# First attention of a two-block kernel: stacked head pairs and score products on 64 rows each

## The reference, cut to what matters

```
qa = partial_rope(rms_norm(q_a.reshape(B, S, 8, 64), moba_q_norm[l]), positions)
ka = partial_rope(rms_norm(k_a.reshape(B, S, 8, 64), moba_k_norm[l]), positions)
s_own = jnp.einsum('bhqd,bhld->bhql', qi, k_own) * 64 ** -0.5
s_own = jnp.where(kpos[None, :] <= qpos[:, None], s_own, -jnp.inf)
p = jax.nn.softmax(s_own, axis=-1)
o_a = jnp.einsum('bhql,bhld->bhqd', p, v)
```

## Time and profile before

| | |
|---|---|
| median of 3 runs | 1429.86 us (1429.76 to 1430.22) |
| span of the profiled execution | 1426.4 us |
| PE busy | 1393.7 us, 98% |
| DVE busy | 990.3 us, 69% |
| ACT busy | 753.3 us, 53% |
| chain that ended last | PE 86%, DVE 7%, ACT 4% |
| mean granted TensorE clock | 0.998 |

### The profile page before, as it was taken

How to read it: one execution, slowest core, us unless ns; L and a number is a source line. 1 busy time by engine, 2 the same in 40 slices (tenths; PEclk the granted TensorE clock), 3 DMA queues, 4 the chain that set the end, 5 groups by cost and what they waited for, 6 DMA issues and landing times.

```text
span 1426.4 us, 18882 instructions
## 1 busy us (share of the span) xinstructions
PE 1393.7 (98%) x7575; PEld 1194.3 (84%) x7575; DVE 990.3 (69%) x1201; ACT 753.3 (53%) x1061; POOL 60.0 (4%) x46
## 2 busy tenths in 40 slices
PE   7999999999999999999999999999999999999998
PEld 6988888988887988898877888879788987788886
DVE  6689777698766679647776565457795568665553
ACT  6764766764764575434454443356743445444432
POOL 2002000002000000000000000000100000000000
PEclk9999999999999999999999999999999999999999
DMA  8544345544333654324445555454533334375553
GB/s 302 189 147 148 96 136 181 175 140 143 108 119 125 236 193 147 119 100 151 143 153 177 178 185 179 154 211 157 199 119 119 108 134 157 118 227 186 177 178 117
DMA packets 139125, 225.72 MB, mean 158 GB/s; under 512 B 8032, under 2 KB 54432, under 8 KB 138912
## 3 DMA queue, kind: packets, MB, share of 16 engines
q1 hardware_dynamic: 137376, 221.90, 46.3%
q10 hardware_dynamic: 1664, 2.63, 0.5%
HBM read 223.46 MB, written 1.05 MB: 157 GB/s over the span
## 4 chain that ended last, share of the span: by engine, by line
PE 86%; DVE 7%; ACT 4%; issue 1%; DMA 1%; POOL 1%; SPq 0%; ACTq 0%; DVEq 0%
PE gp L577 63%; PE gp L566 7%; PE mp L847 5%; PE mp L549 4%; DVE wt_rest L1423 2%; PE mp L684 2%; DVE arena L1417 1%; PE mp L738 1%; DVE arena L1885 1%; POOL rs_out L2130 1%; PE mp L840 1%; PE mp L712 1%; PE mp L698 0%; ACT first_hi L1035 0%; ACT arena L1272 0%
## 5 line engine op out<-in xcount | busy, mean ns | idle before, releaser
L1423 DVE TENSOR_TENSOR wt_rest<-wt,wt_hi 128x1024 fp32r<-128x1024 f32 x156 | 184.0, 1221 | 75.1 <-ACT wt_hi L1035 74.3
L1035 ACT ACTIVATE wt_hi<-wt 128x1024 fp32r<-128x1024 f32 x156 | 156.7, 1054 | 101.0 <-DMA wt<-in_ffn_up 49.7
L1423 DVE TENSOR_TENSOR wt_rest<-wt,mix_hi 128x1024 fp32r<-128x1024 f32 x136 | 160.6, 1221 | 57.9 <-ACT mix_hi L1035 56.9
L1035 ACT ACTIVATE mix_hi<-wt 128x1024 fp32r<-128x1024 f32 x136 | 139.6, 1061 | 101.3 <-PE gp L577 57.0
L577 PE MATMUL gp<-wt_rest,mix_hT_hi 128*128 128x512 f32 x384 | 149.6, 390 | 0.0
L577 PE MATMUL gp<-wt_hi,hT_hi 128*128 128x512 f32 x352 | 140.3, 398 | 4.8 <-DVE wt_rest L1423 4.0
L577 PE MATMUL gp<-mix_hi,mix_hT_hi 128*128 128x512 f32 x352 | 140.6, 399 | 4.1 <-DVE wt_rest L1423 3.0
L577 PE MATMUL gp<-wt_hi,hT_rest 128*128 128x512 f32 x352 | 137.4, 390 | 0.0
L577 PE MATMUL gp<-mix_hi,mix_hT_rest 128*128 128x512 f32 x352 | 137.2, 390 | 0.0
L577 PE MATMUL gp<-wt_rest,hT_hi 128*128 128x512 f32 x352 | 137.1, 390 | 0.0
L1035 ACT ACTIVATE first_hi<-wt 128x1024 fp32r<-128x1024 f32 x104 | 106.4, 1061 | 47.8 <-PE gp L577 36.4
(11 more groups left out here) (320 smaller groups left out, 3028.4 us busy)
## 6 DMA issues: line engine op xcount, KB each, us to landing
wt<-in_w_in SPq DMA_DIRECT2D x100, 1024.0 KB, 4.9
wt<-in_ffn_gate SPq DMA_DIRECT2D x44, 512.0 KB, 3.7
wt<-in_ffn_up SPq DMA_DIRECT2D x44, 512.0 KB, 4.8
wt<-in_w_out SPq DMA_DIRECT2D x20, 1024.0 KB, 4.9
wt<-in_ffn_down SPq DMA_DIRECT2D x20, 1024.0 KB, 4.9
wt<-in_w_mem_kv SPq DMA_DIRECT2D x8, 1024.0 KB, 6.0
wt<-in_w_branch_pool SPq DMA_DIRECT2D x4, 1024.0 KB, 5.0
wt<-in_w_branch_ret SPq DMA_DIRECT2D x4, 1024.0 KB, 5.0
```

Source lines behind the costliest of these rows:

```text
L1035: nc.scalar.activation(rounded_part(u)[:, k:k + nk, :], wt[:, u % SLOTS, k:k + nk, :], ACT.Copy)\
L1423: return nc.vector.tensor_tensor(o, i0, i1, ALU.subtract)
```

## The change

QT gets the layout of KT: 4 pairs, even head in partitions 0 to 63, odd head in 64 to 127, no zeros. ACT copies it in two instructions of 128 partitions in place of four of 64. POOL's zero fill of QT is gone. A score product takes the 64 partitions of its own head, queries and keys. `scores` works on a pair: it begins both heads' steps (the waits of both stand ahead of the first product), then does t = 0 of the even head, t = 0 of the odd head, t = 1 of the even head, t = 1 of the odd head. The order of the steps and of everything else is as before.

```diff
-        QT, KT = region(a_QT, NH_A, S), region(a_KT, 4, S)
+        QT, KT = region(a_QT, 4, S), region(a_KT, 4, S)
...
-                def scores(h):
-                    begin(s(f"sc{h}"), read_out(s("kaT0")), read_out(s("kaT1")), read_out(s("qaT0")), read_out(s("qaT1")))
-                    b = bank(s(f"sc{h}"))
-                    nc.tensor.matmul(b[:, 0:P], QT[:, h, 0:P], KT[:, h // 2, 0:P], start=True, stop=True)
-                    end(nc.tensor.matmul(b[:, P:3 * P], QT[:, h, P:S], KT[:, h // 2, :], start=True, stop=True))
+                def scores(pair):
+                    for h in (2 * pair, 2 * pair + 1):
+                        begin(s(f"sc{h}"), read_out(s("kaT0")), read_out(s("kaT1")), read_out(s("qaT0")), read_out(s("qaT1")))
+                    for t in range(TT):
+                        for h in (2 * pair, 2 * pair + 1):
+                            rows = slice(DH_A * (h % 2), DH_A * (h % 2) + DH_A)
+                            o = bank(s(f"sc{h}"))[:, P * t:P * t + P * (t + 1)]
+                            ins = nc.tensor.matmul(o, QT[rows, pair, P * t:P * t + P], KT[rows, pair, 0:P * (t + 1)], start=True, stop=True)
+                            if t == TT - 1:
+                                end(ins)
...
-                for h in range(4):
-                    scores(h)
+                for pair in range(2):
+                    scores(pair)
                 y_transposes(2)
                 split_units(s("Z0"), 1)
-                for h in range(4, 8):
-                    scores(h)
+                for pair in range(2, 4):
+                    scores(pair)
                 split_units(s("Z0"), 1)
...
-                for t in range(TT):
-                    st = s(f"qaT{t}")
-                    act.wait_ge(*computed(st))
-                    nc.scalar.activation(QT[0:64, 0:8:2, t * P:t * P + P], bank(st, 4, P)[0:64], ACT.Copy)
-                    nc.scalar.activation(QT[64:128, 1:8:2, t * P:t * P + P], bank(st, 4, P)[64:128], ACT.Copy).then_inc(step_read[STEP_NO[st] % 4], 1)
-                for t in range(TT):
-                    evacuate(f"kaT{t}", KT[:, :, t * P:t * P + P], bank(s(f"kaT{t}"), 4, P))
+                for n, dst in (("qaT", QT), ("kaT", KT)):
+                    for t in range(TT):
+                        evacuate(f"{n}{t}", dst[:, :, t * P:t * P + P], bank(s(f"{n}{t}"), 4, P))
...
-            nc.gpsimd.memset(QT, 0.0)
```

## The result

| | before | changed |
|---|---|---|
| median, first comparison | 1429.81 us (4 runs) | 1435.04 us (4 runs, 1434.78 to 1435.70) |
| ratio | | 1.0039, 95% interval 1.0024 to 1.0053 |
| span of the profiled execution | 1426.4 us | 1432.8 us |
| PE, DVE, ACT, POOL busy | 1393.7, 990.3, 753.3, 60.0 | 1394.5, 990.3, 750.4, 59.1 |

The account below looks back on a forecast made before the run. PE was taken as the bound (busy 98%, 86% of the chain). After the last bank's release, 0.11 + 0.88 + 0.10 = 1.09 us against 0.76, +0.33 a layer, +0.7 in two: 1429.86 to 1430.5 us; range 1429.0 to 1432.3.

Parts of the forecast that it names:

- Where the products stand: Scores of heads 0 to 5 lie beside ACT's work; PE's 1.40 us a layer saved there becomes wait.
- ACT's copies and POOL's fill at nothing: ACT's 1.37 us a layer ends in its waits for PE; POOL's 1.80 us at the start is off the path: 0.
- The pair: Two heads' score products on separate halves, partly overlapping, rows starting in order: 0.88 us on PE.
- The middle of my bounds: Pair time of 0.88 us, between 0.66 with perfect overlap and 1.31 with none.
- The change of form: Tile form back from 64 to 128 rows behind heads 6 and 7: 0.10 us a layer, ends 0 and 0.31.
- The order of the waits: Heads 6 and 7 start only when both banks are free, at 178.40 as before; 1.09 us after release, before 0.76.
- The high end of my range: After the release, no overlap and large change of form: 0.11 + 1.31 + 0.31 = 1.73 us, +0.97 a layer.
- The clock: Granted clock behind PE's wait before heads 6 and 7: the sum kept it at 1.00, adding nothing.
- the rival: Longer wait halves the clock behind heads 6 and 7: 1.45 us a layer, 1433.4; chance 0.07 both layers, 0.03 one.

Follow-up runs that it names:

- e11: The changed kernel with POOL's zero fill of the query region put back at the start; 1434.90 us, ratio 1.0034 to before.
- e10: The changed kernel with scores head after head again, each head with its own waits and its own 64 rows; 1432.71 us, ratio 1.0021 to before.
- e2: The changed kernel with six extra full products, results unused, between heads 5 and 6; 1430.87 us, ratio 1.0010 to before.
- e9: The changed kernel with query and key waits only at head 0 and six unused full products between heads 5 and 6; 1429.56 us, ratio 1.0000 to before.
- e3: The changed kernel with the query and key waits only at head 0, not at all eight heads; 1432.28 us, ratio 1.0019 to before.
- e14: As e9, but two full filler products before heads 6 and 7 instead of six; 1431.95 us, ratio 1.0015 to before.
- e5: The kernel before, its 128-row products in the change's order of waits and products, executed once more for a trace; 1434.66 us (1 run).
- e12: As e9, but the six filler products use only the lower 64 rows; 1430.05 us, ratio 1.0003 to before.

## Why the prediction was wrong

**Where the products stand.** Right. The first five or six heads lie beside ACT's work, and all that PE saved there became wait: 5.0 us in two layers.

**ACT's copies and POOL's fill at nothing.** Right: the gain of 1.4 us a layer is in ACT's longer wait, and e11 shows the fill.

**The pair.** The middle of my bounds (0.88) was wrong, the low end (0.66) right. Rows on one half do not hold up the rows on the other (e10 shows it even for heads in a row). On the path that is 0.22 less than I had put there; it also lengthened the wait.

**The change of form.** I took 0.10 with 0 and 0.31 as ends. It is 0.19 a layer, 5.68 and not 5.49 for the unit with the clock at 1.00 (e2, e9).

**The order of the waits.** This step of the sum failed in part. I priced it as the time of the products behind the release and took the release as it was. Measured: 0.56 us between release and first product, where it was 0.05, since the wait for the later bank stands first of five wait instructions (e3: 0.14 with two), and the same lag at heads 2 and 3, where DVE then waited and moved the release by 0.25. I had read in the order that one row carries the waits of both banks, but not which of them comes last. The high end of my range had +0.97 a layer, so this alone (+0.76), and with the form (+0.95, 1.9 us in two layers), would have stayed inside.

**The clock.** This is what put the time outside. The sum holds the granted clock at 1.00 behind the longer wait, so it puts this term at nothing; I had it only as a rival, with 0.07 for both layers, because 2.5 to 2.7 us lay between two idle times of the trace, 1.71 and 3.13. It fell in both layers of every traced execution with such a wait, at 1.59 us a layer in the changed kernel's trace (e11: 1.5 and 2.8, pair and unit against e2's); my price for the rival, 1.45, was near. I had set one row of 1.71 us against it, and e10 and e14 show that even 1.56 and 1.62 us are no safe length. The page "TensorE: Matmul & The Clock Gate" of the Trainium skill, section on HAM oscillation, describes a kernel in which the half clock comes back in each pause between bursts of matmuls. Its pauses are longer (about 3 to 5 us) than the 2.5 us here, so it was a hint and no forecast of this wait.

The section on packing small matmuls of the same page of the Trainium skill, with starts 4 ns apart on different row groups, was also nearer than my model of the pair: the pair's 0.66 agrees with it.

The sum with the measured terms: 2 x (0.25 release + 0.51 lag + 0.19 form + 1.59 clock) = 5.1 us; measured 5.2. That these agree so closely is partly luck, since the medians of e3 and e11 differ from the sums of their own rows by about 1 us.

## What to carry to other kernels

A faster piece of PE work in front of a wait gives nothing, and the longer wait can cost the clock of what follows; look for work to put there before making the piece faster, and then for the engine that leads behind it (here ACT's sigmoid, ahead of copies that PE needed). When two steps' waits are put in front of one instruction, place the one that comes last at the very end, and drop waits that an earlier one has met already. Where a trace has a wait that kept the clock and one that lost it, price everything between as lost when drawing the range; here even waits shorter than the one that kept it lost it elsewhere (1.56 against 1.71 us). When a piece of work moves, ask also whether the release that it waits for moves with it.

## What the runs showed that I had not expected

- Six useless products of 0.23 us each, in each layer, made a kernel 4.2 us faster (e2 against the changed kernel).
- Even and odd heads overlap on the two halves without any alternation in the program: two heads in 0.93 us of rows, four in 1.79 (e10).
- Each wait instruction between a release and the product costs about 0.1 us on PE, an estimate from (0.56 - 0.14) / 4: 0.56 us with the late semaphore first of five, 0.14 us with it first of two (e3), 0.05 us with it last.
- Products on 64 rows, on one half alone, held the clock as full ones did (e12).
- The order of the waits moved the release of the last bank as well, by 0.25 us a layer on 64 rows and by 0.50 on 128 (e5).
